# PEER channel mixer: 64 of the 512 prompt tokens through gathered expert rows, the other 448 dense, and group loads in four parts

## The chip, the cores and the metric

One core of one Trainium2 chip runs the whole program in one launch. The metric is the device time of that launch in microseconds. All computing is in fp32; the large products are made of three fp32r products of a high and a low part each (high times high, high times low, low times high).

## What is computed

Two decoder layers on 512 prompt tokens and 8 sample tokens, with a width of 1024. Each layer is a token mixer (a gated MLP in the first, sparse attention in the second) and then PEER, the part that the change touches:

```python
def _peer(h, w_q, sub_k1, sub_k2, expert_u, expert_v):
    ...
        q = (xb @ w_q).reshape(PEER_BLOCK, PEER_HEADS, 2, PEER_HALF)
        s1 = jnp.einsum('thd,kd->thk', q[:, :, 0], sub_k1).astype(jnp.float32)
        s2 = jnp.einsum('thd,kd->thk', q[:, :, 1], sub_k2).astype(jnp.float32)
        v1, i1 = lax.top_k(s1, PEER_TOPK)
        v2, i2 = lax.top_k(s2, PEER_TOPK)
        ...
        top_s, top_pos = lax.top_k(cand, PEER_TOPK)
        eidx = jnp.take_along_axis(cand_idx, top_pos, axis=-1)
        gate = jax.nn.softmax(top_s, axis=-1)
        u = expert_u[eidx]
        act = jax.nn.gelu(jnp.einsum('thkd,td->thk', u, xb))
        vv = expert_v[eidx]
        return jnp.einsum('thk,thkd->td', (gate * act).astype(vv.dtype), vv)
```

Each token has 8 heads, and each head picks 16 of 16384 experts. An expert is one row of `expert_u` and one of `expert_v`, 1024 numbers (4 KB) each.

## The kernel before, in words

The prompt tokens don't gather. For them the kernel computes all 16384 experts densely, since 512 tokens of 128 choices each touch most of them anyway, and multiplies the result by a gate that is zero where an expert was not chosen. The work goes by **slabs**: a slab is 128 experts by 1024, so `expert_u` and `expert_v` have 128 slabs each per layer, and every other weight matrix is cut in slabs too. SyncE (SP) loads slab after slab into four buffers `raw`; ScalarE (ACT) copies one into `w_hi` (`split`, line 937), GpSimd (POOL) subtracts to get `w_lo` (line 1897), and TensorE (PE) makes 24 matmuls of it (8 pieces of the contraction, 3 products), in `dense` (line 517) with 512 token columns each, in `slab` (line 504) with 2 x 260. `w_hi` and `w_lo` have two buffers each, so ACT and POOL work one slab ahead of PE.

A layer's PEER has two stages.

**Stage s** (u rows, 128 slabs): PE's result of a slab goes through the gelu on ACT (line 1045) to HBM (`act_d`). Between slabs the routing runs, for four blocks of 128 tokens: VectorE (DVE) finds the best keys and experts (`routing`) beside 12 slabs of PE, PE turns the result round (line 681), and then 16 slabs follow with a step of gates each: DVE makes one-hot rows of 8 tokens (lines 1535 and 1536), PE multiplies them into the 128 x 128 gate table of each token (`gates`, line 637), ACT evicts it (line 1058), and SP stores it (`gate_d`). 12 + 16 slabs by four blocks are 112; 16 slabs without gates end the stage. The 8 sample tokens are gathered: in blocks 1 and 2 POOL fetches rows of u, then of v, by an indirect DMA (line 1931; 64 rows: 8 heads by 8 tokens), and DVE makes the dot product (line 1512) or adds the weighted row (line 1524).

**Stage y** (v rows, 128 slabs in 16 groups of 8): for each group ACT issues two loads, the activations `abuf` and the gates `gbuf` (lines 1067 and 1069), DVE multiplies them (`weigh`, line 1606), ACT and POOL split the product into `y_hi` and `y_lo` (lines 1081 and 1962; the second set of buffers is `h_hi` and `h_lo`), and PE multiplies with the v slabs; DVE adds each result into `x` (line 1621). The group ahead is prepared while PE works on the present one. The first group is loaded and split at the end of stage s (`load_first`, `hi_part`, `low_part`).

The order on each engine is the order of the code; semaphores alone tie the engines together. What sets the order around the change is written out by hand: the last slabs of stage s and `y_group` on ACT, POOL and DVE:

```python
def hi_part(j, c, par):
    act.wait_ge(y_mult, j * GRP + (W0 + c + 1))
    act.activation(y_hi[par][:, c, 0:TP], abuf[par][:, c, :], ACT.Copy).then_inc(y_hi_done, 1)
```

Of the kernel before, what the change touches and what calls it, by code (L numbers as in the profile page):

```python
# [111 lines left out]
def build(nc, a, outs, layers=2):  # L112
# [3 lines left out]
    with es:  # L116
# [30 lines left out]
        sel_t = sb("sel_t", [SR, TS])  # L147
        ms_at = place[0]
# [58 lines left out]
        idxT = take("idxT", [P, 2, TP])  # L207
        gateT = take("gateT", [P, TP])
# [13 lines left out]
        qS = take("qS", [P, 2, SR])  # L222
        y_tail = take.end
        gelu = take("gelu", [P, 2, TP])
# [5 lines left out]
        rows_at = take.end  # L230
        rows = [take(f"rows{r}", [P, D]) for r in range(2)]
        h_rows = take("h_rows", [P, D])
        v_sum = take("v_sum", [P, D])
        hS = at("hS", [P, KC, SR], F32, ms_at)
# [133 lines left out]
        v_sum_done, s_y_done, s_y_added = sem("v_sum_done"), sem("s_y_done"), sem("s_y_added")  # L368
        stored = sem("stored")
# [31 lines left out]
        N_CONST = 9  # L401
# [4 lines left out]
        def _(sp):  # L406
# [18 lines left out]
            def peer_loads(l, last):  # L425
# [23 lines left out]
                for b in range(4):  # L449
                    steps(12)  # L450
                    q1 = done[0] // 4
                    with sp.Fori(q1, q1 + P // HG // 4, 1) as q:
# [5 lines left out]
                    done[0] += P // HG  # L458
# [30 lines left out]
        def _(pe):  # L489
# [20 lines left out]
            def dense(n, r, par, m_hi, m_lo, free, made=None):  # L510
# [105 lines left out]
            def peer(l):  # L616
# [30 lines left out]
                for j in range(2):  # L647
                    last = pe.matmul(acc[0:SR, 1, 0, j * P:(j + 1) * P], qS[:, j, :], subk[:, 2 * l + j, :],
                                     start=True, stop=True)
                last.then_inc(s_sc_done, 1)  # L650
                for c in range(KC):
                    last = pe.transpose(acc[0:SR, c // 4, 1, (c % 4) * P:(c % 4 + 1) * P], hS[:, c, :], ident[:])
                last.then_inc(h_rows_done, 1)

                for b, (t0, w) in enumerate(BLOCK[:NDB]):
                    B = l * NDB + b
                    if b == 3:
# [3 lines left out]
                        for c in range(KC):  # L661
                            last = pe.matmul(acc[:, 0, 1, c * TS:(c + 1) * TS], v_sum[0:SR, c * P:(c + 1) * P],
# [1487 lines left out]
```

## Time and profile before

| | |
|---|---|
| device time, median of 3 runs | 4435.58 us (4430.29 to 4436.59) |
| the profiled execution's own time | 4438.91 us |
| its span, first to last instruction | 4437.1 us |
| busy PE, DVE, ACT, POOL | 94%, 46%, 32%, 45% |
| mean granted TensorE clock | 0.973 of full speed |
| moved by DMA | 659.83 MB, mean 149 GB/s |

Busy time is the time in which an engine executes at least one instruction; matmuls overlap each other, so the mean length of one (about 0.4 us) is longer than the distance from one to the next, and the distance is what counts. "Idle before" is the time for which an engine stood still ahead of an instruction, with what released it. The queue's own rows (ACTq, SPq) show how long an issue kept the engine's instruction stream.

### The profile page before, as it was taken

The numbers are of one execution on the slowest core, as the hardware profiler recorded it, in microseconds if no ns is written. First come the engines' busy times: TensorE is split into PE (matmuls) and PEld (weight loads), VectorE is DVE, ScalarE is ACT, GpSimd is POOL, SyncE is SP. The second block draws the span as 40 slices with busy tenths as digits, with TensorE's granted clock in tenths as the row PEclk, the third lists the DMA queues.
The fourth block names the chain that finished last, engine by engine and source line by source line (L and its number), as shares of the span: only waits on it lengthen the run. The fifth ranks groups of instructions, "written<-read, shape, count | busy, mean of one in ns | idle before, by whom it ended". The sixth has DMA issues, their size and how long they took to land.

```text
span 4437.1 us, 65563 instructions
## 1 busy us (share of the span) xinstructions
PE 4182.9 (94%) x21677; PEld 3461.8 (78%) x21677; DVE 2052.0 (46%) x5322; ACT 1437.1 (32%) x1929; POOL 1997.9 (45%) x1004
## 2 busy tenths in 40 slices
PE   7899999999998999999887799999999998999998
PEld 7898887878886888887853458887878887888887
DVE  2332567989722222222556432567989721222221
ACT  2222343434432333332220332343434432333332
POOL 3333334444335666665520003334444335666664
PEclk9999999999999999999997899999999999999999
DMA  3122344645457565652134222344645457565652
GB/s 119 67 72 71 105 161 151 205 154 189 146 180 227 183 196 182 201 177 93 62 114 144 74 65 72 102 161 145 206 154 193 148 176 228 187 193 185 198 180 81
DMA packets 345165, 659.83 MB, mean 149 GB/s; under 512 B 22008, under 2 KB 186616, under 8 KB 336248
## 3 DMA queue, kind: packets, MB, share of 16 engines
q1 hardware_dynamic: 163152, 488.74, 32.2%
q10 hardware_dynamic: 176096, 149.67, 11.5%
q0 software_dynamic: 5776, 19.72, 1.9%
q8 instruction: 66, 1.08, 0.1%
q14 instruction: 75, 0.61, 0.0%
HBM read 520.44 MB, written 137.61 MB: 148 GB/s over the span
## 4 chain that ended last, share of the span: by engine, by line
PE 88%; DVE 4%; issue 4%; POOL 2%; ACT 1%; ACTq 0%; DMA 0%; SPq 0%; POOLq 0%; DVEq 0%
PE acc L517 61%; PE acc L504 14%; PE misc L637 5%; PE misc L842 1%; PE acc L856 1%; POOL w_lo L1897 1%; PE misc L879 1%; PE misc L527 1%; PE misc L784 1%; PE acc L868 1%; DVE passed L1733 1%; PE misc L672 1%; DVE sq L1340 1%; DVE hot_gate L1536 0%; DMA unit<-ck_in 0%
## 5 line engine op out<-in xcount | busy, mean ns | idle before, releaser
L1897 POOL TENSOR_TENSOR w_lo<-raw,w_hi 128x1024 fp32r<-128x1024 f32 x620 | 1539.5, 2484 | 2207.5 <-ACT w_hi L937 2207.5
L517 PE MATMUL acc<-h_hi,w_hi 128*128 128x512 f32 x3072 | 1233.0, 401 | 25.9 <-POOL w_lo L1897 25.6
L517 PE MATMUL acc<-h_hi,w_lo 128*128 128x512 f32 x3072 | 1220.0, 397 | 0.0
L517 PE MATMUL acc<-h_lo,w_hi 128*128 128x512 f32 x3072 | 1213.7, 395 | 0.0
L937 ACT ACTIVATE w_hi<-raw 128x1024 fp32r<-128x1024 f32 x620 | 656.9, 1060 | 1310.5 <-PE acc L517 897.5
L517 PEld LDWEIGHTS acc<-h_hi,w_hi 128*128 128x128 f32 x3072 | 579.8, 189 | 164.6 <-issue 35.2
L517 PEld LDWEIGHTS acc<-h_hi,w_lo 128*128 128x128 f32 x3072 | 579.8, 189 | 139.2
L517 PEld LDWEIGHTS acc<-h_lo,w_hi 128*128 128x128 f32 x3072 | 580.8, 189 | 133.7
L1621 DVE TENSOR_TENSOR x<-x,acc 128x512 f32<-128x512 f32 x256 | 176.0, 687 | 1087.2 <-PE acc L517 1087.2
L1045 ACT ACTIVATE gelu<-acc 128x512 f32<-128x512 f32 x256 | 152.9, 597 | 969.3 <-PE acc L517 969.2
L1535 DVE TENSOR_SCALAR hot<-acc,idxT 128x128 f32<-128x128 f32 x1024 | 344.3, 336 | 244.9 <-PE misc L637 129.6
L517 PE MATMUL acc<-y_hi,w_hi 128*128 128x512 f32 x1024 | 402.0, 393 | 29.7 <-POOL y_lo L1962 16.4
L1536 DVE TENSOR_SCALAR hot_gate<-acc,idxT,gateT 128x128 f32<-128x128 f32 x1024 | 405.5, 396 | 0.0
L517 PE MATMUL acc<-y_lo,w_hi 128*128 128x512 f32 x1024 | 401.2, 392 | 0.0
L517 PE MATMUL acc<-y_hi,w_lo 128*128 128x512 f32 x1024 | 400.9, 391 | 0.0
L504 PE MATMUL acc<-h_hi,w_hi 128*128 128x260 f32 x1472 | 311.5, 294 | 79.2 <-DVE h_lo L1343 30.0
L504 PEld LDWEIGHTS acc<-h_hi,w_hi 128*128 128x128 f32 x1472 | 233.5, 194 | 94.3 <-issue 74.0
L504 PE MATMUL acc<-h_hi,w_lo 128*128 128x260 f32 x1472 | 302.8, 288 | 0.0
L504 PE MATMUL acc<-h_lo,w_hi 128*128 128x260 f32 x1472 | 302.6, 288 | 0.0
L1606 DVE TENSOR_TENSOR abuf<-abuf,gbuf 128x512 f32<-128x512 f32 x256 | 181.4, 713 | 225.1 <-DMA gbuf<-gate_d 225.1
L1058 ACT ACTIVATE gout<-misc 128x512 f32<-128x512 f32 x256 | 250.6, 1058 | 35.7 <-PE misc L637 35.7
L637 PEld LDWEIGHTS misc<-hot_gate,hot 128*128 128x128 f32 x2048 | 247.5, 191 | 15.9 <-issue 5.2
(307 smaller groups left out, 4454.1 us busy)
## 6 DMA issues: line engine op xcount, KB each, us to landing
raw<-slabs_in SPq DMA_DIRECT2D x620, 512.0 KB, 3.5
act_d<-gelu SPq DMA_DIRECT2D x256, 256.0 KB, 2.1
gate_d<-gout SPq DMA_DIRECT2D x64, 1024.0 KB
abuf<-act_d ACTq DMA_DIRECT2D x32, 2048.0 KB, 10.9
gbuf<-gate_d ACTq DMA_DIRECT2D x32, 2048.0 KB, 19.0
unit<-cv_in SPq DMA_DIRECT2D x128, 128.0 KB, 2.0
unit<-ck_in SPq DMA_DIRECT2D x64, 160.0 KB, 3.1
unit<-ck_in ACTq DMA_DIRECT2D x64, 160.0 KB, 3.1
```

The costliest lines, as they stand in the source:

```text
L504: last = pe.matmul(acc[:, par, half, 0:HT], w[:, c, :], m(c)[:, half * HT:(half + 1) * HT], start=start and c == 0 and w is w_hi[r] and m ...
L517: last = pe.matmul(acc[:, par, 0, :], w[:, c, :], m(c)[:, 0:TP], start=c == 0 and w is w_hi[r] and m is m_hi, stop=c == KC - 1 and w is w_ ...
L527: last = pe.matmul(misc[:, half, 0:HT], ones[:], sq[:, c, half * HT:(half + 1) * HT], start=c == 0, stop=c == KC - 1)
L637: last = pe.matmul(misc[:, q, j * P:(j + 1) * P], hot1[par][:, t, :], hot_gate[par][:, t, :], start=True, stop=True)
L937: act.activation(w_hi[r % 2][:], raw[r][:], ACT.Copy).then_inc(hi_done, 1)
L1045: act.activation(gelu[:, par, :], acc[:, par, 0, :], ACT.Gelu_apprx_tanh).then_inc(acc_free_act, 1)
L1058: act.activation(gout[cpar][:, :, t0:t0 + 4].rearrange("p i t -> p t i"), misc[:, q, :].rearrange("p (t i) -> p t i", t=4), ACT.Copy).then ...
L1535: dve.tensor_scalar(hot1[par][:, t, :], count_row, idxT[:, 0, t0 + t:t0 + t + 1], None, ALU.is_equal)
L1536: last = dve.tensor_scalar(hot_gate[par][:, t, :], count_row, idxT[:, 1, t0 + t:t0 + t + 1], gateT[:, t0 + t:t0 + t + 1], ALU.is_equal, AL ...
L1606: dve.tensor_tensor(abuf[par][:, c, :].rearrange("p (n t) -> p n t", t=TG), abuf[par][:, c, :].rearrange("p (n t) -> p n t", t=TG), gbuf[p ...
L1621: dve.tensor_tensor(x[:, c, 0:TP], x[:, c, 0:TP], acc[:, c % 2, 0, :], ALU.add).then_inc(acc_free_dve, 1)
L1897: pool.tensor_tensor(w_lo[r % 2][:], raw[r][:], w_hi[r % 2][:].bitcast(F32), ALU.subtract).then_inc(lo_done, 1)
```

## The change

The last 64 prompt tokens (448 to 511) leave the dense path. `ND` is 448: every matmul of `dense`, every gelu, `weigh`, split and addition now has 448 columns, `act_d` and `gate_d` are that much smaller, and block 3 has 8 steps of gates instead of 16 (`STEPS_OF`). The 64 tokens are `NSG` = 4 groups of 16 tokens by 8 heads, 128 partitions. For each group POOL fetches 16 times 128 rows of u and 16 times 128 rows of v into four buffers `rows_p`; the first comes 24 slabs before the end of stage s, and from then on one fetch follows each slab. DVE makes one product with a fetched row per slab (`group_dot`, `group_value`), with the group's tokens, or its sum, in PSUM. The low part of y moves from POOL to DVE (`low_part`). ACT loads a group in four parts, one every second slab, and in stage s it loads the first two groups together. The loops of stage y are written out.

```diff
+ND = 448
+NSG = (TP - ND) // TG
+NG = ND // TG
+RB = 4
...
+                        steps(8)
+                        sp.wait_ge(route_done, l * NDB + 4)
+                        sp.dma_start(route_d[l].rearrange("g t k h s -> (g t) k h s"),
+                                     route[P - NSG * TG:P]).then_inc(p_route_stored, 16)
+                        steps(4)
+                        sp.wait_ge(p_route_stored, 16 * (l + 1))
+                        for g in range(NSG):
+                            for h in range(PH):
+                                sp.dma_start(routeP[h * TG:(h + 1) * TG, g], route_d[l][g, :, :, h]).then_inc(
+                                    p_route_loaded, 16)
...
-                        last = pe.matmul(acc[:, par, 0, :], w[:, c, :], m(c)[:, 0:TP],
+                        last = pe.matmul(acc[:, 0, par, 0:ND], w[:, c, :], m(c)[:, 0:ND],
...
+                def group_h(g):
+                    pe.wait_ge(p_hS_done, l * NSG + g + 1)
...
+                    for c in range(KC):
+                        last = pe.transpose(acc[:, 1, c // 4, (c % 4) * P:(c % 4 + 1) * P], hSP[:, c, :], ident[:])
+                def group_y(g):
+                    pe.wait_ge(p_v_out_done, l * NSG + g + 1)
+                    for c in range(KC):
+                        last = pe.matmul(misc[:, 2, c * TG:(c + 1) * TG], v_out[:, c * P:(c + 1) * P], sel_p[:],
+                                         start=True, stop=True)
...
+                def load_part(j, par, part):
+                    k = part % 2
+                    if part < 2:
+                        act.dma_start(gbuf[par][:, k * NG // 2:(k + 1) * NG // 2],
...
                 def load_first():
                     for par in range(2):
-                        act.wait_ge(act_stored[par], (l * NK // 2 + GRP // 2 + 1) * 16)
+                        act.wait_ge(act_stored[par], (l * NK // 2 + 2 * GRP // 2 + 1) * 16)
                         act.wait_ge(gate_stored[par], ((l + 1) * NG // 2 + 1) * 16)
                     load_group(0, 0)
+                    load_group(1, 1)
...
                 s_only(8)
                 load_first()
-                s_only(4)
+                s_only(8)
+                group_act(0)
+                s_only(NK - 4 - done[0])
...
+            def group_dot(l, g, k):
...
+                dve.wait_ge(p_rows_loaded[i % RB], 16 * (i // RB + 1))
+                row = rows_p[i % RB]
+                dve.tensor_tensor_reduce(out=row[:].rearrange("p (k d) -> p k d", k=2), in0=acc[:, 1],
+                                         in1=row[:].rearrange("p (k d) -> p k d", k=2), scale=1.0, scalar=0.0,
+                                         op0=ALU.mult, op1=ALU.add, accum_out=dotP[:, k:k + 1]).then_inc(p_rows_used, 1)
+            def group_value(l, g, k):
...
+                    dve.wait_ge(p_rows_used, i)
+                    dve.scalar_tensor_tensor(total, row, weightP[:, k:k + 1], total, ALU.mult, ALU.add).then_inc(
+                        p_rows_used, 1)
...
+                for i in range(TOPK):
+                    sparse(i)
                 for c in range(GRP):
-                    weigh(0, 0, c, 0)
+                    weigh(0, c)
+                for c in range(GRP):
+                    sparse(TOPK + c)
+                    low_part(0, c)
...
+                    if TAIL + n < NSG * 2 * TOPK:
+                        sparse(TAIL + n)
+                    if j + 1 < J:
+                        low_part(j + 1, c)
...
+                def group_fetch(i):
+                    g, k = divmod(i, 2 * TOPK)
+                    n = l * NSG * 2 * TOPK + i
+                    if n >= RB:
+                        pool.wait_ge(p_rows_used, n - RB + 1)
...
+                    if n == done:
+                        pool.wait_ge(p_expert_done, l + 1)
+                        for par in range(2):
+                            pool.wait_ge(gate_stored[par], ((l + 1) * NG // 2 + 1) * 16)
+                    while fetched < min(n - done + 3, NSG * 2 * TOPK):
+                        group_fetch(fetched)
+                        fetched += 1
```

How the rows of an engine stand, in three places. The first is DVE in stage y, over one slab, before (`abuf` and `gbuf` are the group's activations and gates, `acc` is PSUM):

```order
L1621 TENSOR_TENSOR x<-x,acc 128x512
L1606 TENSOR_TENSOR abuf_140<-abuf_140,gbuf_141 128x512
L1618 REGISTER_ALU
L1620 REGISTER_ALU
L1621 TENSOR_TENSOR x<-x,acc 128x512
```

and now:

```order
L1789 TENSOR_TENSOR x<-x,acc 128x448
L1745 TENSOR_TENSOR abuf_149<-abuf_149,gbuf_150 128x448
L1645 SCALAR_TENSOR_TENSOR misc<-rows_p_148,weightP,misc 128x1024
L1752 TENSOR_TENSOR h_lo<-abuf_149,h_hi 128x448
L1789 TENSOR_TENSOR x<-x,acc 128x448
```

The product with a fetched row (`misc` is PSUM, `rows_p_148` one of the four row buffers) and the low part stand between `weigh` and the next addition into `x`.

The second is POOL near the end of stage s, now, where the first rows are fetched; before, only the rows of `w_lo` stood here, and `y_lo` behind them:

```order
L2059 TENSOR_TENSOR w_lo_60<-raw_54,w_hi_58 128x1024
L2124 DMA rows_127<-u_in,expertP 128x1024
L2124 DMA rows_128<-u_in,expertP 128x1024
L2124 DMA rows_p_148<-u_in,expertP 128x1024
L2059 TENSOR_TENSOR w_lo_59<-raw_55,w_hi_57 128x1024
L2124 DMA rows_p_151<-u_in,expertP 128x1024
L2059 TENSOR_TENSOR w_lo_60<-raw_56,w_hi_58 128x1024
```

Three fetches follow the first split, and one each of the next 125.

The third is ACT at `load_first`, before (eight slabs behind the last step of gates, and eight ahead of stage y):

```order
L937 ACTIVATE w_hi_57<-raw_53 128x1024
L1042 REGISTER_ALU
L1045 ACTIVATE gelu<-acc 128x512
L1048 REGISTER_ALU
L1048 COMPARE_AND_BRANCH
L1067 DMA abuf_136<-act_d 128x8x512
L1069 DMA gbuf_137<-gate_d 128x32x128
```

and now:

```order
L1002 ACTIVATE w_hi_57<-raw_53 128x1024
L1108 REGISTER_ALU
L1111 ACTIVATE gelu<-acc 128x448
L1114 REGISTER_ALU
L1114 COMPARE_AND_BRANCH
L1135 DMA gbuf_145<-gate_d 128x14x128 x2
L1140 DMA abuf_144<-act_d 128x4x448 x2
L1135 DMA gbuf_150<-gate_d 128x14x128 x2
L1140 DMA abuf_149<-act_d 128x4x448 x2
```

Two loads have become eight, ahead of the next split on ACT; the loads of the second group stood behind the last split of stage s before.

## Rows read from the trace of the kernel before

**Rows 1.** The page, part 1 (busy time) and part 4 (chain that ended last), whole span.

```profile
PE 4182.9 (94%) x21677; PEld 3461.8 (78%) x21677; DVE 2052.0 (46%) x5322; ACT 1437.1 (32%) x1929; POOL 1997.9 (45%) x1004
PE 88%; DVE 4%; issue 4%; POOL 2%; ACT 1%; ACTq 0%; DMA 0%; SPq 0%; POOLq 0%; DVEq 0%
```

**Rows 2.** Stretches: us, busy (x) PE, PEld, DVE, ACT, POOL, PEclk, DMA share, GB/s.

```profile
404.06:490.81 86.75, 86.73 (x720) 86.53 (x720) 9.79 (x14) 14.86 (x14) 35.57 (x15) 1.00 0.28 94
1276.96:1360.68 83.72, 83.72 (x362) 67.57 (x361) 7.11 (x8) 23.69 (x31) 36.58 (x15) 1.00 0.61 203
1400.00:2090.00 690.00, 690.00 (x3002) 562.54 (x3001) 156.29 (x242) 208.23 (x248) 454.02 (x243) 1.00 0.55 174
800.00:840.00 40.00, 40.00 (x224) 34.29 (x223) 40.00 (x100) 18.89 (x23) 17.31 (x11) 1.00 0.62 201
1322.00:1342.00 20.00, 20.00 (x88) 16.12 (x87) 0.00 (x0) 5.94 (x8) 9.11 (x4) 1.00 0.98 318
```

**Rows 3.** Chain of waits, stage s with gates: start us, us, what.

```profile
1210.54 5.59 PE acc L517 x24
1216.14 1.78 PE misc L637 x16
```

**Rows 4.** Timeline of ACT, DVE, POOL, one slab of stage y.

```profile
1804.40 1.06 ACT L937 ACTIVATE w_hi<-raw 128x1024 fp32r<-128x1024 f32 x1 [3.60 <-PE acc L517]
1804.43 0.69 DVE L1621 TENSOR_TENSOR x<-x,acc 128x512 f32<-128x512 f32 x1 [4.29 <-PE acc L517]
1805.03 0.68 DVE L1606 TENSOR_TENSOR abuf<-abuf,gbuf 128x512 f32<-128x512 f32 x1
1805.54 2.44 POOL L1897 TENSOR_TENSOR w_lo<-raw,w_hi 128x1024 fp32r<-128x1024 f32 x1 [1.84 <-ACT w_hi L937]
1807.94 1.28 POOL L1962 TENSOR_TENSOR y_lo<-abuf,y_hi 128x512 fp32r<-128x512 f32 x1
```

**Rows 5.** Timeline of DVE and POOL where they meet: stage s, block 1, and first weigh.

```profile
770.94 1.21 DVE L1512 CUSTOM_DVE_ANT_0 v_sum<-rows,h_rows 64x1024 f32<-64x1024 f32 x1
...
804.76 2.39 POOL L1897 TENSOR_TENSOR w_lo<-raw,w_hi 128x1024 fp32r<-128x1024 f32 x1 [2.74 <-ACT w_hi L937]
805.11 0.39 DVE L1536 TENSOR_SCALAR hot_gate<-acc,idxT,gateT 128x128 f32<-128x128 f32 x1
805.42 2.81 DVE L1512 CUSTOM_DVE_ANT_0 v_sum<-rows,h_rows 64x1024 f32<-64x1024 f32 x1
...
1386.34 2.34 POOL L1897 TENSOR_TENSOR w_lo<-raw,w_hi 128x1024 fp32r<-128x1024 f32 x1 [12.23 <-ACT w_hi L937]
1386.88 2.34 DVE L1606 TENSOR_TENSOR abuf<-abuf,gbuf 128x512 f32<-128x512 f32 x1 [35.98 <-DMA gbuf<-gate_d]
```

**Rows 6.** Timeline from stage s to stage y: ACT's issues, and PE's waits.

```profile
1374.30 8.88 ACTq L1067 DMA_DIRECT2D abuf<-act_d  x1
1383.33 1.65 ACTq L1069 DMA_DIRECT2D gbuf<-gate_d  x1
1385.20 1.06 ACT L937 ACTIVATE w_hi<-raw 128x1024 fp32r<-128x1024 f32 x1 [16.25 <-issue]
...
1374.44 0.79 PE L517 MATMUL acc<-y_hi,w_hi 128*128 128x512 f32 x1 [8.20 <-POOL y_lo L1962]
1388.94 0.79 PE L517 MATMUL acc<-y_hi,w_hi 128*128 128x512 f32 x1 [6.99 <-POOL w_lo L1897]
```

**Rows 7.** DMA issues: queue, count, KB each, median us from issue to landing.

```profile
gbuf<-gate_d ACTq DMA_DIRECT2D x32, 2048.0 KB, 19.0
rows<-u_in,expert POOLq DMA_INDIRECT x32, 4.2
```

**Rows 8.** Timeline of PE and DVE, routing of block 3 beside twelve slabs.

```profile
1086.19 0.48 PE L517 MATMUL acc<-h_hi,w_hi 128*128 128x512 f32 x1
...
1139.75 0.79 PE L517 MATMUL acc<-h_hi,w_hi 128*128 128x512 f32 x1 [3.06 <-POOL w_lo L1897]
1144.58 0.29 DVE L1482 TENSOR_TENSOR route<-route,gsum 128x128 f32<-128x128 f32 x1
```

More of the change, by code:

```diff
@@ L147, in build @@
         sel_t = sb("sel_t", [SR, TS])
+        sel_p = sb("sel_p", [P, TG])
         ms_at = place[0]
@@ L222, in build @@
         qS = take("qS", [P, 2, SR])
+        idxT = take("idxT", [P, 2, ND])
+        gateT = take("gateT", [P, ND])
         y_tail = take.end
-        gelu = take("gelu", [P, 2, TP])
+        gelu = take("gelu", [P, 2, ND])
+        gates_at = take.end
         HG = TG // 2
@@ L228, in build @@
         gout = [take(f"gout{r}", [P, P, TG]) for r in range(2)]
-        rows_at = take.end
+        gates_end = take.end
         rows = [take(f"rows{r}", [P, D]) for r in range(2)]
@@ L233, in build @@
         v_sum = take("v_sum", [P, D])
+        h_sp = at("h_sp", [P, KC, NSG * TG], F32, take.end - 2 * 4 * D)
+        v_out = v_sum
+        routeP = take("routeP", [P, NSG, 3, TOPK])
+        expertP = take("expertP", [P, NSG, TOPK], U32)
+        dotP = take("dotP", [P, TOPK])
+        dot_actP = take("dot_actP", [P, TOPK])
+        weightP = take("weightP", [P, TOPK])
+        hSP = at("hSP", [P, KC, P], F32, ms_at)
         hS = at("hS", [P, KC, SR], F32, ms_at)
@@ L1954, in peer @@
                     done += P // HG
-                plain(q0 + done // 4, (NK - 4 - done) // 4)
-                done = NK - 4
-                W0 = l * NK
-                J = NK // GRP
-                def low_part(j, c, par):
-                    pool.wait_ge(y_hi_done, j * GRP + (W0 + c + 1))
-                    pool.tensor_tensor(y_lo[par][:, c, 0:TP], abuf[par][:, c, :], y_hi[par][:, c, 0:TP].bitcast(F32),
-                                       ALU.subtract).then_inc(y_lo_done, 1)
-                for r in range(4):
-                    ahead(q0 + done // 4, r)
-                    if r >= 2:
-                        for c in range(GRP // 2):
-                            low_part(0, (r - 2) * GRP // 2 + c, 0)
@@ L1971, in peer @@
-                yq0 = BASE[f"y{l}"] // 4
-                def y_group(j, par, last):
-                    for c in range(GRP):
-                        ahead(j * 2 + (yq0 + c // 4), c % 4, last=l == LAST_L and last and c == GRP - 1)
-                        if not last:
-                            low_part(j + 1, c, 1 - par)
-                with pool.Fori(0, J - 2, 2) as j:
-                    y_group(j, 0, False)
-                    y_group(j + 1, 1, False)
-                y_group(J - 2, 0, False)
@@ new lines, in peer @@
+                fetched = 0
+                for n in range(done, 2 * NK):
+                    ahead(q0 + n // 4, n % 4, last=l == LAST_L and n == 2 * NK - 1)
+                    if n == done:
[5 more added lines that the diff above has]
+                        fetched += 1
```

251 lines of the change are left out of this document (171 added, 80 removed).

## The prediction

> **What bounds the kernel now.** I read the page first, then stretches of each stage, then the chain and the timelines where stages meet. PE is busy for 94% of the span and holds 88% of the chain that ended last [rows 1]. The stretches say how: in 690 us of stage y PE issues 3002 matmuls without a gap, one per 0.230 us, 5.52 us for the 24 of a slab; in the last fifteen plain slabs of stage s it is 83.72 us / 15 = 5.58 us [rows 2]. A slab with gates adds 1.78 us, in 16 records of 0.111 us [rows 3]. So what counts is PE's column count, as long as every other engine finishes within a slab. In stage y they do: ACT splits 1.06 us, POOL 2.44 + 1.28 us, DVE 0.69 + 0.68 us [rows 4]. Little else stops PE; where it stands still, I count it below.
>
> A difference of under 0.2%, 9 us, a measurement of this kernel can't tell from none. The profiled execution took 4438.9 us; the sum is made against it, and the median of the runs shown is 3 us lower.
>
> **The columns.** All 512 slabs of both stages in both layers go from 512 to 448 columns. At 260 columns a matmul follows another after 86.75 us / 720 = 0.1205 us, at 512 after 83.72 / 360 = 0.2326 us [rows 2]. Between them lies 0.000445 us per column, so 64 columns are worth 0.0285 us, 24 matmuls 0.68 us: a slab takes 4.90 us in stage s and 4.84 us in stage y. 512 x 0.68 = **-350 us**. Strict proportion would give 0.70 us and -356.
>
> The Trainium skill (VectorE: DVE Perf Modes, on the TRN2 errata) gives a matmul 6 cycles plus one per column at 2.4 GHz: 64 columns would be 0.0267 us and the term an estimated -328. By its formula 512 columns are 0.216 us; the trace has 0.2326, so I go by the trace's slope.
>
> **The gates.** Block 3 has 8 steps less per layer: 16 x 1.78 = **-28 us** [rows 3]. Their slabs stay, as plain ones.
>
> **PE's new work.** Four groups per layer, each with 8 transposes and 8 small matmuls. The nearest rows are the fp32 matmuls of the gates, 0.111 us per record, two records each [rows 3]: at most 16 x 0.222 = 3.6 us, at least half, since a transpose or 16 columns may need less. I take 2.5 us, eight times: **+20 us** (14 to 28).
>
> **From stage s to stage y.** Before, PE waits 8.20 us for the first `y_lo` and 6.99 us for a `w_lo` [rows 6]. The second wait is ACT's: with one group's loads outstanding, the next issue held its queue 8.88 us, the one behind it 1.65 us, and `w_hi` came 16.25 us late. Each time the matmuls after the wait come at half speed (0.79 us the first) for some 3 us, 1.5 us lost. Together 18 us a layer. Now that wait moves rather than goes. `load_first` issues both groups, eight parts, between two splits. Two groups were 8.4 MB, and are 7.3 MB now, so I scale the 15.9 us between ACT's last split and its next to 12 to 13 us. Then 1.06 us `w_hi` and 2.4 us `w_lo` follow, against a slab of 4.9 us in progress: PE waits about 11 us, half speed behind it. If the queue takes smaller parts without holding, eight issues of about 0.5 us each cost nothing to 3 us.
> At the stage's end a new wait follows from the order of DVE: its second value row stands behind `low_part(0, 0)`, which needs `y_hi` of slab 124; POOL's fetch of row 21 waits for that value before POOL splits the next slab. From slab 124's end that is gelu 0.6, `y_hi` 0.6, `low_part` 0.6, value 1.2, then `w_lo` 2.4 us: PE waits some 5.5 us. And group 0 is complete only when DVE has made its last two low parts and a value, about 4 us after slab 127. 11 + 5.5 + 4 + three restarts of 1.5 = 25 to 26 us against 18: **+16 us** for both layers (-30 to +40).
>
> **POOL's wait for the gate stores.** Before the first fetches POOL waits for the last 1 MB gate store, issued about 2 us after PE's last gates step, and then issues three fetches of 0.9 us or more. The next `w_lo` is due within that slab: 3 to 5 us of PE per layer, **+8 us** (0 to 16).
>
> **Block 3 and SP.** SP now waits for `route_done` after 8 of the 12 slabs. DVE finishes routing 58.4 us after PE's first matmul of the block [rows 8]. Twelve new slabs take 58.8 us, so DVE is just in time, where it had 14 us. But SP stands at that wait with the gelu stores of slabs 8 and later and the load of slab 12 behind it; gelu 10 needs store 8 landed. That makes slab 12 late by 2 to 7 us: **+10 us** for two layers. The 32 small loads of `routeP` (0.35 us each as SP issues, 11 us) pass beside two slabs with gates. DVE's copy and sum of the 64 tokens ahead of the first one-hot rows, 2 us, and the first step of gates in each block now shows behind a shorter slab: **+10 us**.
>
> **Routing collisions.** POOL's `w_lo` is held by a long DVE instruction, and PE waits 3.06 us [rows 8]. With 0.68 us less per slab, each of eight blocks loses about 1 us more: **+8 us**.
>
> **DVE and POOL in stage y.** DVE gets a product of 128x1024 and the low part. The price of the product is the question. Alone, the sample dot takes 1.21 us; started beside POOL's `w_lo` (804.76 to 807.15) it takes 2.81, from 805.42 to 808.23, which is the wait for POOL's end plus its own time. `weigh` does the same at 1386.88. One-hot rows, whose big input is PSUM, keep 0.39 us beside POOL [rows 5]. So two SBUF inputs wait for POOL, and the change keeps the other operand of the product in PSUM: 1.2 to 1.3 us, in any place. DVE per slab: 0.55 + 0.6 + 1.25 + 0.55 = 2.95 us, of which `weigh` runs before POOL starts (1.1 us into the slab) and `low_part` after it ends (3.6 us): done at 4.2 us of 4.84. POOL: 2.44 + fetch 0.9 (64 rows) to 1.8 us. Both fit. The slack of 0.6 us fails at some group ends, where PE needs all low parts, above all because `weigh` runs twice in a group's first slab: 0.6 us each in 32 groups, **+20 us** (0 to 60).
> The Trainium skill (SBUF — State Buffer, Who interferes with whom) has this as a rule: a VectorE instruction with two SBUF inputs and a GpSimd one that reads SBUF exclude each other for a whole instruction, one SBUF input does not. The rows agree.
>
> **Sum.** -350 - 28 + 20 + 16 + 8 + 10 + 10 + 8 + 20 = -286: 4438.9 - 286 = 4153, less 3 for the median: **4150 us**, chance 0.50.
>
> **The rivals.**
> *The stalls shrink.* The queue takes the small parts, and the transition gets better than before (-30), the group ends fit (0), the small terms halve: about -365, **4075 to 4100**. For it: parts of 0.9 MB; against it: the 8.88 us [rows 6]. Chance 0.17.
> *DMA is the bound of stage y.* A slab now needs 512 KB of weights, 512 KB of rows, and 448 KB of group: 1.51 MB in 4.84 us, 311 GB/s, where 174 are moved now. With everything queued, the trace holds 318 GB/s for 20 us at a share of 0.98 [rows 2], with more small packets than later. The present group takes 19 us to land [rows 7]; a fetch has about 7 us from issue to use, and 64 rows land in 4.2. At 285 GB/s a slab is 5.29 us: 208 slabs x 0.45 = +94, **4245 us** (300 GB/s: +39; 265 GB/s: +176). Chance 0.20.
> The Trainium skill (DMA: Bandwidth & Descriptors, Specifications) puts HBM at about 358 GB/s per core; by that 311 fits, at 87%.
> *The product waits for POOL after all (slower).* If the custom dot, or a sum that is read and written in PSUM, needs the same port, all of `w_lo` 2.44, `weigh` 0.6, the product 1.2, `low_part` 0.55 and the fetch 0.9 to 1.8 us exclude each other: 5.7 to 6.6 us, and with a hand-over between two in-order engines at each step 6.5 us. Then 208 slabs x 1.66 = +345: **4495 us**. From 6.2 us per slab on the change loses. For it: the product was never run on PSUM in this trace; against it: the one-hot rows. Chance 0.08.
> *It doesn't buy columns.* If 128 weight rows at 0.188 us per load were the floor rather than the columns, 448 columns would save nothing: about 4500 us. Against it: 260 columns follow at 0.1205. Chance 0.01; the rest, 0.04, is for mixtures above 4300.
>
> **The numbers.** Range 4080 to 4290: it holds the likeliest case with its bounds, most of the first rival, and the DMA case to 270 GB/s. Faster by over 0.2%: 0.89, within: 0.02, slower: 0.09.
>
> **What would show it.** Plain slabs of stage s at 4.9 us; 16 gate records gone from 16 steps; the product at 1.2 to 1.3 us beside POOL; ACT's queue held for about 12 us at `load_first`, with one PE wait of 11 us; PE busy in stage y with gaps at group ends only. I am wrong if stage y's slabs come at over 5.1 us, with DVE waiting for rows or parts (DMA) or with products of over 2 us (the port).

## The result and the profile after

The changed kernel takes **4130.39 us** (median of 4 runs, 4124.94 to 4132.71). The kernel before took 4436.09 us beside it (4 runs, 4430.29 to 4442.36). The ratio is 0.9309, with a 95% interval of 0.9293 to 0.9325: 306 us less. The profiled execution took 4132.7 us, its span is 4130.9 us, and the mean granted TensorE clock is 0.967.

The page of the changed kernel, parts 1 and 4, answers to [rows 1]:

```profile
PE 3827.7 (93%) x21613; PEld 3464.5 (84%) x21613; DVE 2661.3 (64%) x5734; ACT 1366.3 (33%) x1913; POOL 1954.2 (47%) x1004
PE 81%; DVE 7%; issue 5%; POOL 2%; ACT 2%; SPq 1%; DMA 1%; ACTq 0%; POOLq 0%; DVEq 0%
```

PE's busy time fell by 4182.9 - 3827.7 = 355.2 us. The time in which PE is idle rose from 4437.1 - 4182.9 = 254.2 to 4130.9 - 3827.7 = 303.2 us. So PE's smaller work brings 355 us, and 49 us of new waits are taken off it.

Two stretches of the changed kernel, stage s without gates and stage y, answer to [rows 2]. Columns: us, busy (x) of PE, PEld, DVE, ACT, POOL, PEclk, DMA share, GB/s.

```profile
1230.00:1275.00 45.00, 45.00 (x223) 41.64 (x222) 15.61 (x19) 14.11 (x21) 30.61 (x18) 1.00 0.82 257
1600.00:1680.00 80.00, 80.00 (x402) 74.50 (x401) 68.32 (x70) 25.57 (x33) 59.44 (x34) 1.00 0.90 310
```

PE is busy without a gap in both. In y DVE is busy for 68.32 of 80 us, and the DMA engines move 310 GB/s where they moved 174. One slab of y in the changed kernel, timeline of DVE and POOL, answers to [rows 4]:

```profile
1450.84 2.69 DVE L1745 TENSOR_TENSOR abuf<-abuf,gbuf 128x448 f32<-128x448 f32 x1
1453.45 1.28 DVE L1645 SCALAR_TENSOR_TENSOR misc<-rows,weightP,misc 128x1024 f32<-128x1024 f32 x1
1454.64 0.61 DVE L1752 TENSOR_TENSOR y_lo<-abuf,y_hi 128x448 fp32r<-128x448 f32 x1
1455.18 0.61 DVE L1789 TENSOR_TENSOR x<-x,acc 128x448 f32<-128x448 f32 x1
1455.71 2.69 DVE L1745 TENSOR_TENSOR abuf<-abuf,gbuf 128x448 f32<-128x448 f32 x1
...
1450.64 2.41 POOL L2059 TENSOR_TENSOR w_lo<-raw,w_hi 128x1024 fp32r<-128x1024 f32 x1 [1.16 <-ACT w_hi L1002]
1453.20 1.16 POOL L2124 DMA_INDIRECT rows_p<-v_in,expertP  x1 [0.15 <-issue]
```

From one `weigh` to the next are 4.87 us: that is a slab. `weigh` starts 0.2 us behind `w_lo`, lasts until POOL has ended, and ends 0.48 us after that. The product that follows has its sum in PSUM and takes 1.28 us.

The new waits stand where the stages meet. Timeline of ACT and of PE in the first layer, end of stage s, answering to [rows 6]:

```profile
1194.56 1.35 ACTq L1135 DMA_DIRECT2D gbuf<-gate_d  x2
1195.94 7.80 ACTq L1140 DMA_DIRECT2D abuf<-act_d  x2
1203.77 6.63 ACTq L1135 DMA_DIRECT2D gbuf<-gate_d  x2
1210.43 4.35 ACTq L1140 DMA_DIRECT2D abuf<-act_d  x2
1215.06 1.06 ACT L1002 ACTIVATE w_hi<-raw 128x1024 fp32r<-128x1024 f32 x1 [20.22 <-issue]
...
1218.77 0.74 PE L554 MATMUL acc<-h_hi,w_hi 128*128 128x448 f32 x1 [19.64 <-POOL w_lo L2059]
```

`load_first`'s eight issues keep ACT for 20 us. `w_hi` comes late, `w_lo` behind it, and PE stands 19.64 us (19.96 in the second layer). Some 65 us later, in the last slabs of stage s, timelines of DVE, POOL and PE:

```profile
1280.33 0.62 DVE L1752 TENSOR_TENSOR y_lo<-abuf,y_hi 128x448 fp32r<-128x448 f32 x1 [19.15 <-ACT y_hi L1158]
1280.87 1.28 DVE L1645 SCALAR_TENSOR_TENSOR misc<-rows,weightP,misc 128x1024 f32<-128x1024 f32 x1
...
1282.42 1.08 POOL L2124 DMA_INDIRECT rows<-v_in,expertP  x1 [8.92 <-DVE misc L1645]
1283.53 2.35 POOL L2059 TENSOR_TENSOR w_lo<-raw,w_hi 128x1024 fp32r<-128x1024 f32 x1
...
1286.11 0.74 PE L554 MATMUL acc<-h_hi,w_hi 128*128 128x448 f32 x1 [6.86 <-POOL w_lo L2059]
...
1300.33 0.46 PE L554 MATMUL acc<-h_hi,w_hi 128*128 128x448 f32 x1 [2.00 <-POOL w_lo L2059]
```

DVE's second value stands behind a low part that waits for ACT's `y_hi`; POOL's fetch waits for the value, and the split of the next slab for the fetch. A last place is block 3, where SP first waits for `route_done` and then issues the 32 loads of `routeP`, timelines of SP and PE:

```profile
1092.07 20.95 SPq L486 DMA_DIRECT2D routeP<-route_d  x32
...
1092.24 0.46 PE L554 MATMUL acc<-h_hi,w_hi 128*128 128x448 f32 x1 [3.84 <-POOL w_lo L2059]
```

### The profile page after: what moved, and what is told of

Its sections match the earlier page's. It is cut to its first block, busy times and chain, and to the rows that moved or that the text cites. A ratio compares the mean times of both kernels' runs of the same rounds, so it can differ in the third digit from the quotient of the medians.

```text
span 4130.9 us, 64131 instructions
## 1 busy us (share of the span) xinstructions
PE 3827.7 (93%) x21613; PEld 3464.5 (84%) x21613; DVE 2661.3 (64%) x5734; ACT 1366.3 (33%) x1913; POOL 1954.2 (47%) x1004
## 4 chain that ended last, share of the span: by engine, by line
PE 81%; DVE 7%; issue 5%; POOL 2%; ACT 2%; SPq 1%; DMA 1%; ACTq 0%; POOLq 0%; DVEq 0%
PE acc L554 52%; PE acc L541 15%; PE misc L674 5%; POOL w_lo L2059 2%; PE misc L907 1%; PE acc L921 1%; SPq L486 1%; PE misc L849 1%; PE misc L944 1%; PE misc L564 1%; PE acc L933 1%; DVE passed L1895 1%; DMA act_d<-gelu 1%; PE misc L709 1%; DVE sq L1423 1%
## 5 line engine op out<-in xcount | busy, mean ns | idle before, releaser
L554 PE MATMUL acc<-h_hi,w_hi 128*128 128x448 f32 x3072 | 1143.9, 372 | 100.3 <-POOL w_lo L2059 100.3
L554 PE MATMUL acc<-h_hi,w_lo 128*128 128x448 f32 x3072 | 1130.7, 368 | 0.0
L554 PE MATMUL acc<-h_lo,w_hi 128*128 128x448 f32 x3072 | 1127.2, 367 | 0.0
L554 PEld LDWEIGHTS acc<-h_hi,w_lo 128*128 128x128 f32 x3072 | 582.9, 190 | 47.7
L554 PEld LDWEIGHTS acc<-h_lo,w_hi 128*128 128x128 f32 x3072 | 584.0, 190 | 45.6
L1111 ACT ACTIVATE gelu<-acc 128x448 f32<-128x448 f32 x256 | 139.3, 544 | 852.8 <-PE acc L554 806.2
L554 PE MATMUL acc<-y_hi,w_hi 128*128 128x448 f32 x1024 | 372.4, 364 | 5.2 <-DVE y_lo L1752 5.2
L554 PE MATMUL acc<-y_lo,w_hi 128*128 128x448 f32 x1024 | 372.6, 364 | 0.0
L554 PE MATMUL acc<-y_hi,w_lo 128*128 128x448 f32 x1024 | 371.8, 363 | 0.0
L1789 DVE TENSOR_TENSOR x<-x,acc 128x448 f32<-128x448 f32 x256 | 158.5, 619 | 223.8 <-PE acc L554 207.6
L541 PEld LDWEIGHTS acc<-h_lo,w_hi 128*128 128x128 f32 x1472 | 233.6, 194 | 0.0
L541 PEld LDWEIGHTS acc<-h_hi,w_lo 128*128 128x128 f32 x1472 | 232.9, 193 | 0.0
```

What stands on the lines that cost most here:

```text
L541: last = pe.matmul(acc[:, par, half, 0:HT], w[:, c, :], m(c)[:, half * HT:(half + 1) * HT], start=start and c == 0 and w is w_hi[r] and m ...
L554: last = pe.matmul(acc[:, 0, par, 0:ND], w[:, c, :], m(c)[:, 0:ND], start=c == 0 and w is w_hi[r] and m is m_hi, stop=c == KC - 1 and w is ...
L1111: act.activation(gelu[:, par, :], acc[:, 0, par, 0:ND], ACT.Gelu_apprx_tanh).then_inc(acc_free_act, 1)
L1789: dve.tensor_tensor(x[:, c, 0:ND], x[:, c, 0:ND], acc[:, 0, c % 2, 0:ND], ALU.add).then_inc(acc_free_dve, 1)
```

## The experiments

All twelve start from the changed kernel and alter one thing, or join such alterations. Times are medians; the ratio is to the kernel before, measured beside each (its medians: 4433.6 to 4435.0 us).

**1. Loads of the first groups spread out (load_spread).**

The edit, shortened:

```diff
 load_first()    # now without its two load_group calls
-load_group(0, 0); load_group(1, 1)    # they stood in load_first
-s_only(8)
+for i in range(8):
+    s_step(done[0] // 4 + i // 4, i % 4)
+    load_part(i // 4, i // 4, i % 4)
```

> Edit: the eight loads with which ScalarE fetches groups 0 and 1 of a layer go out one after each of the next eight slabs of the s stage instead of all in a row; nothing else changes. Theory 1 (ScalarE's queue is held by its own loads): in the changed kernel TensorE stands 19.64 us (first layer) and 19.96 us (second) before the matmul at 1218.77, while ScalarE's issues and weight truncations in that place take 1.35, 7.80, 6.63 and 4.35 us plus 20 us of idle put down to issue. Spread out, each load has a slab of 4.87 us to go, the gap falls to under 3 us in both layers, and the time is 4130 - 2 x (17 to 19) = 4092 to 4097 us. Theory 2 (the loads move as fast as the DMA engines allow, whoever issues them, and the wait only moves to where the group is first used): a new gap of 10 to 20 us shows before the first slabs of y, and the time stays within 4120 to 4132 us.

Measured: 4100.18 us, ratio 0.9249 (0.9235 to 0.9263), 30 us less. ACT and PE in its timeline:

```profile
1204.36 5.20 ACTq L1140 DMA_DIRECT2D abuf<-act_d  x1
...
1213.40 0.47 PE L554 MATMUL acc<-h_hi,w_hi 128*128 128x448 f32 x1 [4.21 <-ACT w_hi L1002]
```

Nothing new shows at the start of y (2.61 us, as without the edit). ACT's queue was the cause. One load in each slab is still too many: the third, activations behind two loads of gates, holds ACT for 5.20 us.

**2. Values ahead of the low parts (values_first).**

```diff
 for c in range(GRP):
     sparse(TOPK + c)
+for c in range(GRP):
     low_part(0, c)
```

> Edit: at the end of the s stage VectorE adds the eight weighted rows 16 to 23 of group 0 first and then makes the eight low parts of dense group 0; in the changed kernel it takes them in turns. Theory 1 (the turns tie the fetches on GpSimd to ScalarE's last slabs: a fetch waits for a row to come free, the row for a low part ahead of it, that for y_hi, that for the last gelus): the gap of 6.86 us before the matmul at 1286.11 goes in each layer, and the restart at half clock behind it; time 4130 - 2 x (6 to 9) = 4112 to 4118 us. Theory 2 (the low parts are then late at the start of y, 8 x 0.6 us in a row on VectorE): the 2.61 us before 1310.49 grow to 6 to 9 us and the time stays at 4125 to 4135 us.

Measured: 4099.92 us, ratio 0.9247 (0.9234 to 0.9259), 30 us less, about twice what I expected. The wait of 6.86 us is gone, 0.30 us is left of the one of 2.00, and 2.24 us are left before y (2.61 before). From the end of `load_first`'s wait to the first matmul of y PE now takes 78.6 us instead of 91.7, and 79.1 instead of 92.8 in the second layer: 27 us less, of which 17 are waits and the other 9 to 10 are the clock. What is left of the 30 lies outside of the edit's reach and is not explained. Timeline of PE in the **changed** kernel:

```profile
1286.11 0.74 PE L554 MATMUL acc<-h_hi,w_hi 128*128 128x448 f32 x1 [6.86 <-POOL w_lo L2059]
1286.64 0.57 PE L554 MATMUL acc<-h_lo,w_hi 128*128 128x448 f32 x1
...
1291.46 0.37 PE L554 MATMUL acc<-h_hi,w_hi 128*128 128x448 f32 x1
1291.67 0.37 PE L554 MATMUL acc<-h_lo,w_hi 128*128 128x448 f32 x1
...
1301.26 0.57 PE L554 MATMUL acc<-h_lo,w_hi 128*128 128x448 f32 x1
1301.63 0.57 PE L554 MATMUL acc<-h_hi,w_lo 128*128 128x448 f32 x1
```

Behind the long wait the matmuls come every 0.37 us instead of 0.20, up to 1291; behind the wait of 2.00 us the clock falls a second time, 0.9 us after the matmuls have begun again. The granted clock is 0.50 from 1286 to 1290 and 0.66 from 1300 to 1305: 1.2 GHz for 4.6 and for some 3.5 us. It falls a third time behind the wait before y. In all 31 matmuls come at the slow distance here, and 8 in run 2. So such a wait costs its length and 1.5 to 2 us more, but not each does: behind the 2.37 us before 547.61 us the matmuls keep the full clock, and behind the 2.37 us before 1071.63 us the clock falls in the changed kernel and doesn't in run 2.

**3. Routes in eight stores and one load (route).**

The edit, shortened (the layout of `route_d` and DVE's wait for the loads change with it):

```diff
-steps(8); wait route_done; 1 store [g, t, k, h, s]; steps(4); 32 loads
+steps(12)
+sp.wait_ge(route_done, l * NDB + 4)
+for h in range(PH):
+    sp.dma_start(route_d[l][:, h], route[P - NSG * TG:P, :, h, :]).then_inc(p_route_stored, 16)
+sp.dma_start(routeP[:], route_d[l].rearrange("g h t k s -> (h t) g k s")).then_inc(p_route_loaded, 16)
```

> Edit: the 64 tokens' routes go out to DRAM in eight stores that already put the heads in order, behind 12 slabs of block 3 instead of 8, and come back in one load in place of 32. Theory 1 (SyncE's queue decides here: it stood 3.84 us for the routing at 1092.24, and the 32 small loads held it for 20.95 us, in which slab 1123.81 waited for its store): the gap of 3.84 us goes, those at 1119.39 and 1123.81 (0.58 and 2.38) go or shrink to the 2.4 us of the other blocks, and the time falls by 2 x (4 to 7) us to 4116 to 4122 us. Theory 2 (the eight stores with 32-byte pieces and the wait for them hold SyncE as long as the 32 loads did): no change, 4127 to 4133 us.

Measured: 4114.17 us, ratio 0.9282 (0.9269 to 0.9294), 16 us less, slightly more than expected. SP's rows in its timeline:

```profile
1084.90 4.03 SPq L481 DMA_DIRECT2D route_d<-route  x7
1090.54 0.40 SPq L483 DMA_DIRECT2D routeP<-route_d  x1
```

The 20.95 us are gone and so are PE's waits of 3.84, 0.58 and 2.38 us in the block; one of 1.97 us before a gates step is new. From the last wait ahead of the block's end (1071.63 us in the changed kernel) to the one behind it the run takes 6.6 us less, and 6.0 in the second layer; 9 of these 12.6 us are waits. The other 3 to 4 us of the 16 are not explained; the stretch up to 1071.63 us, which no edit touches, took 5.2 us less in this profiled execution.

**4. The three together (three).**

> Edit: the edits of load_spread, values_first and route together. If the three waits are independent, the gains add: 2 x (18 + 7 + 5) = 60 us, 4070 us (4058 to 4082). If they are one wait that passes from one place to the next, the sum is under 60 per cent of what the three bring alone, and the time stays above 4090 us. If TensorE's matmul stream were not the bound of the stages, gaps of over 1 us would show inside the slabs of y, where the changed kernel has none.

Measured: 4061.13 us, ratio 0.9155 (0.9142 to 0.9167). Alone they bring 30, 30 and 16, 76 in all; together 69, over 90% of it: the waits are independent but for 7 us.

**5. The product with both operands in SBUF (dot_sbuf).**

The edit, shortened; the sums are then of row times row, and everything else stays:

```diff
-dve.tensor_tensor_reduce(out=row, in0=acc[:, 1], in1=row, ...
+dve.tensor_tensor_reduce(out=row, in0=row,       in1=row, ...
```

> Edit: the product of a fetched row with the token's vector takes the row twice, both operands from SBUF, in place of PSUM and SBUF (the sums are then of row times row; everything else is as before). The question is what the operand in PSUM buys. Theory 1 (a VectorE instruction with two SBUF operands and GpSimd's split or fetch do not run together, one with an operand in PSUM does): a slab of y with a dot then has 2.41 (w_lo) + 1.16 (fetch) + 0.54 + 0.54 (weigh, low part) + 1.2 (dot) = 5.85 us one after the other against 4.87 us of matmuls; 48 such slabs in each layer give 96 x 1.0 = 96 us more, 4215 to 4280 us. Theory 2 (where the operands lie does not matter here, the order of the queues alone does): 4125 to 4140 us.

Measured: 4136.65 us, ratio 0.933 (0.9316 to 0.9344), 6 us more, with intervals that still overlap (the changed kernel's ends at 0.9325). The mechanism of theory 1 is there, its price is not. DVE and POOL in its timeline, stage y:

```profile
1399.98 1.21 DVE L1625 CUSTOM_DVE_ANT_0 rows_p<-rows_p 128x1024 f32<-128x1024 f32 x1
1405.12 3.42 DVE L1625 CUSTOM_DVE_ANT_0 rows_p<-rows_p 128x1024 f32<-128x1024 f32 x1
...
1399.95 3.49 POOL L2059 TENSOR_TENSOR w_lo<-raw,w_hi 128x1024 fp32r<-128x1024 f32 x1
1404.89 2.56 POOL L2059 TENSOR_TENSOR w_lo<-raw,w_hi 128x1024 fp32r<-128x1024 f32 x1
```

One of the two now waits for the other: at 1400 the split takes 3.49 us beside a product of 1.21, at 1405 the product 3.42. Over y the mean product takes 2.04 us instead of 1.22. So the operand in PSUM does keep the product and the split apart. Only the products with u rows were edited, 96 of them in y; the 112 with v rows kept their sum in PSUM. But the slab holds it: without the fetch the exclusive pieces are 2.41 + 0.54 + 0.54 + 1.21 = 4.70 us, under 4.87. My 5.85 had counted the fetch, 1.16 us, as one of them; run 8 shows places where it isn't, this run also fetches of 1.76 us that start within such a product.

**6. One load every second slab (spread_two).** Like run 4, with `s_only(4)` ahead of `load_first` and `load_part` after every second of the next 16 slabs.

> Edit: like three, but the eight loads start four slabs earlier and go out one every second slab. In load_spread TensorE still stood 4.21 and 4.87 us, since the third load (of 896 KB) took ScalarE 5.20 us to issue. Theory 1 (a slab of s with a fetch moves 512 KB of weights, 224 KB of acts and 512 KB of rows, 1.25 MB; a load more in every slab makes 2.14 MB in 4.87 us, 440 GB/s, above the 300 to 400 the trace shows at its highest; one every second slab makes 1.7 MB, 348 GB/s): the gap of 5 us goes or falls under 2 us in both layers, 4061 - 2 x (4 to 7) = 4047 to 4053 us. Theory 2 (group 1 then lands too late for the first slabs of y): the gap turns up at the start of y, 4060 to 4075 us.

Measured: 4044.50 us, ratio 0.9123 (0.9111 to 0.9136), 86 us under the changed kernel. Each of the eight issues now takes 0.37 to 0.42 us, and from slab 108 to the start of y PE waits 0.30 us once; the wait before y's first matmul stays (2.67 us).

**7. Without the sparse work (no_sparse).** All calls of `group_fetch`, `sparse`, `group_h`, `group_act`, `group_out`, `group_y`, `group_add` and `group_rows` are left out.

> Left out: everything that is done for the 64 sparse tokens behind their routes (fetches, products, gelus, the transposes and the last matmuls on TensorE, the additions), so that their rows of the output lack the layer's part. Theory 1 (TensorE's columns bound both stages and the sparse work lies beside them): the distance of the matmuls in y stays 0.203 us and a slab 4.87 us; the time falls only by TensorE's own new work (8 groups x 2.6 = 21 us) and by the waits at the end of s (2 x 15, as values_first showed) and in the group changes: 4060 to 4080 us. Theory 2 (the fetches or VectorE's products slow the slabs of y): slabs of y get under 4.8 us and the time falls under 4040 us.

Measured: 4076.77 us, ratio 0.9197 (0.9183 to 0.9211): 54 us under the changed kernel. The slabs of y gain nothing beyond PE's own work: from 1400 to 1800 us PE is busy without a gap in both, and a slab takes 4.83 to 4.84 us on average, once PE's transposes and sums are taken off, with rows, products and 307 GB/s as without them and with 204. The wait for `load_first` stays. ACT and PE in its timeline:

```profile
1188.34 6.86 ACTq L1135 DMA_DIRECT2D abuf<-act_d  x2
...
1210.19 0.74 PE L554 MATMUL acc<-h_hi,w_hi 128*128 128x448 f32 x1 [18.63 <-POOL w_lo L2040]
```

There is no fetch here, so the fetches don't cause it.

**8. Fewer columns in y (y384).** `dense` of stage y takes `0:384` instead of `0:ND`; nothing else changes.

> Left out: the matmuls of y run over 384 of the 448 dense columns, so that 64 tokens get no sum; all loads, splits, weighings and sparse work stay. The question is what bounds y next. From 512 to 448 columns the distance of the matmuls went from 0.230 to 0.203 us, so 384 columns would be 0.176 us and a slab 4.22 us. Theory 1 (VectorE and the DMA engines have room for that): 256 x 0.65 = 166 us less, 3960 to 3970 us. Theory 2 (GpSimd and VectorE take turns: 2.41 + 1.16 + 0.54 + 0.54 = 4.65 us in each of the 104 slabs a layer that still have sparse work): 208 x 0.22 + 48 x 0.65 = 77 us less, about 4053 us. Theory 3 (the DMA engines, which moved 306 GB/s in y, have no more): slabs with a fetch stay at 4.87 us, only the 48 others gain, about 4099 us.

Measured: 4024.75 us, ratio 0.9071 (0.9056 to 0.9085), 106 us less: between theories 1 and 2. The distance of the matmuls is 0.175 us and most slabs take 4.21 us, as theory 1 has it; the rest is lost at the group changes. Its waits from 1400 to 1800 us (us in total, times, longest) and two rows of its timelines of POOL and DVE:

```profile
PE acc L554 <- DVE h_lo L1752: 9.0, 6, 2.1
PE acc L554 <- DVE x L1789: 6.0, 12, 0.7
DVE rows_p L1625 <- DMA rows_p<-u_in,expertP: 13.2, 9, 2.2
...
1514.82 0.95 POOL L2124 DMA_INDIRECT rows_p<-u_in,expertP  x1
1515.09 0.08 DVE L1625 DVE_READ_ACCUMULATOR2_ANT dotP<- 128x1 f32 x1
1515.09 0.62 DVE L1752 TENSOR_TENSOR y_lo<-abuf,y_hi 128x448 fp32r<-128x448 f32 x1
```

Theory 2 falls as a floor of 4.65 us in each slab: the low part at 1515.09 runs wholly beside a fetch, and takes its own 0.62 us. What comes next is DVE at the group changes, and behind it the rows, for which DVE now waits up to 2.2 us while 329 GB/s are moved at a DMA share of 0.95 (1400 to 1600 us). Whether the rows are late because the DMA engines are nearly full, no run settles. Theory 3 falls too.

**9. The four loads of a group in a burst (burst).**

```diff
-if j + 2 < J and c % 2 == 0:
-    load_part(j + 2, par, c // 2)
+if j + 2 < J and c == 0:
+    load_group(j + 2, par)
```

> Edit: in y the four loads of a later group go out all before its first slab instead of one every second slab; the rest is as in the changed kernel. Theory 1 (ScalarE is held when it issues loads faster than they land): the weights and rows of a slab take 1.04 MB in 4.87 us, 213 GB/s, of the 300 to 400 seen, so four loads of 0.9 MB need 20 to 30 us; ScalarE is free again when the third and fourth have room, 5 to 10 us late, in each of 14 groups of 2 layers: 140 to 280 us more, 4270 to 4410 us. Theory 2 (ScalarE's one or two slabs of lead and the queue's depth take them, as they did with the two loads per group of the kernel before): 4125 to 4140 us.

Measured: 4366.14 us, ratio 0.9839 (0.9822 to 0.9856), 236 us more: theory 1, within its range. ACT's rows for one group in its timeline:

```profile
1406.83 1.29 ACTq L1135 DMA_DIRECT2D gbuf<-gate_d  x2
1408.15 7.12 ACTq L1140 DMA_DIRECT2D abuf<-act_d  x2
1415.38 1.06 ACT L1002 ACTIVATE w_hi<-raw 128x1024 fp32r<-128x1024 f32 x1 [11.08 <-issue]
```

PE then stands 4.6 to 7.5 us in each group, and its busy time rises by 61.6 us for the same matmuls, since the clock falls behind each such wait.

**10. Two whole loads, gates first (two_whole).** `load_group` issues `gbuf[par][:]` and then `abuf[par][:]`, in y at `c == 0` and in `load_first`; DVE waits for 32 in place of 64.

> Edit: the four loads of a group are two again (gates whole, activations whole, 1.8 MB each), both before the group's first slab, as in the kernel before; at the end of s the four loads of groups 0 and 1 go out in a row. Theory 1 (the queue counts bytes or descriptors that have not landed): at the end of s ScalarE is held as long as with eight parts, 18 to 20 us, and in y it is held in each group as with the burst of four parts, 4270 to 4410 us. Theory 2 (it counts issues): the wait at the end of s falls under 5 us and y has none, 4130 - 30 = 4095 to 4105 us. Theory 3 (it is held only by loads behind two others): the end of s stays at 18 to 20 us, y has no wait, 4125 to 4140 us.

Measured: 4327.23 us, ratio 0.9759 (0.9741 to 0.9777): theory 1's range, though bytes and pieces aren't told apart yet. ACT in its timeline:

```profile
1444.64 0.38 ACTq L1145 DMA_DIRECT2D gbuf<-gate_d  x1
1445.05 7.41 ACTq L1147 DMA_DIRECT2D abuf<-act_d  x1
```

**11. The same two loads, activations first (act_first).** Run 10 with the two issues exchanged: the order of the kernel before.

> Edit: two_whole with the order turned: activations whole first, gates whole second, as the kernel before has them. In two_whole the gates (3584 pieces of 512 B) were issued in 0.4 us and held the activations behind them (1024 pieces of 1792 B) for 7.4 to 8.1 us; in the kernel before, activations then gates took 0.38 and 0.47 us. Theory 1 (it is the number of small pieces ahead in the queue that holds the next issue; with the gates last nothing stands behind them until the next group, 39 us later): both issues of a group take under 1 us in y, TensorE waits for nothing there, and the end of s still stands 8 to 20 us for group 1: 4100 to 4140 us. Theory 2 (it is the bytes outstanding, 3.6 MB at a time): y is held as in two_whole, 4320 us. Theory 3 (the issues are free but the burst crowds out the weights of the next slabs, since rows need the engines too now): TensorE waits for w_hi or w_lo behind a late raw slab, 4150 to 4250 us.

Measured: 4120.53 us, ratio 0.9292 (0.9278 to 0.9306): theory 1. ACT in its timeline, stage y and end of s:

```profile
1460.84 0.37 ACTq L1145 DMA_DIRECT2D abuf<-act_d  x1
1461.24 0.61 ACTq L1147 DMA_DIRECT2D gbuf<-gate_d  x1
...
1191.52 0.59 ACTq L1147 DMA_DIRECT2D gbuf<-gate_d  x1
1192.14 12.17 ACTq L1145 DMA_DIRECT2D abuf<-act_d  x1
```

The same bytes in the other order cost 207 us less. What follows the gates (3584 pieces of 512 B) at once is held; what follows the activations (1024 pieces of 1792 B) is not. With the gates last, only an issue soon behind them pays: the one at 1192.14 is held until 12.8 us after the gates went out. Bytes outstanding are ruled out. Whether it is the number of the pieces, their size or the way in which `gate_d` is read isn't told apart, since all three change with the order.

**12. Whole loads at two places (whole_two_places).** Run 11 with the edits of runs 2 and 3, group 0 loaded behind slab 108 and group 1 behind slab 116.

> Edit: spread_two with whole loads in place of parts: group 0 (activations, gates) behind slab 108, group 1 behind slab 116, later groups before their first slab, and the order of the values and the routes as in three. If the number of small pieces ahead is what holds ScalarE and the bursts crowd out nothing, this simpler version comes to the 4044 us of spread_two (4040 to 4050). If the bursts delay raw slabs or rows in y, it stays above 4060 us. If bytes outstanding hold it, 4230 us.

Measured: 4047.68 us, ratio 0.9133 (0.9121 to 0.9146), the same as run 6 within the intervals. Stretch of stage y:

```profile
1400.00:1800.00 400.00, 400.00 (x2008) 372.74 (x2007) 326.16 (x361) 127.33 (x169) 284.74 (x157) 1.00 0.88 303
```

No part of a group has to be loaded by itself: the order of two loads does what four parts and an issue every second slab did.

## Why the prediction was right, and where its steps were not

The time, 4130 us, is 20 us under the forecast of 4150 and in its likeliest case. The large term, the columns, came out by its mechanism. That the small terms also met is in part luck: the transition cost twice what was forecast, and 28 us of forecast waits were not there. By its steps:

- **The columns** (-350): right. The slab is 4.87 us in stage s and 4.80 to 4.88, on average 4.84, in y; forecast were 4.90 and 4.84: 256 x (5.58 - 4.87) + 256 x (5.52 - 4.84) = 356 us. With the gates (-28) and PE's new work (+20) I had -358; PE's busy time fell by 355, with more matmuls at half clock in it. The -328 by the Trainium skill's formula (VectorE: DVE Perf Modes) would have been 28 us short for the columns.
- **PE's new work** (+20): right, a group's transposes hold the next slab's matmuls for 0.79 us and its sums for 1.70, 8 x 2.5 = 20.
- **The transition** (+16): the mechanism was right, `load_first` was sized wrongly. I scaled 15.9 us by bytes and wrote 12 to 13 (by 7.3 and 8.4 MB it is 13.8); ACT is held 20.2 us and PE 19.64 instead of 11. The step that failed is "two groups were 8.4 MB, and are 7.3 MB now". Runs 10 and 11 show that not bytes count but what stands ahead of an issue: the gates' many small pieces. All waits of the transition and the stage's end are 62.6 us for both layers, where they were 30.4: +32 without the restarts, inside the stated -30 to +40. The rival in which the small parts are taken without holding fell with the changed kernel's 20.2 us and with run 1's 5.20; with the order of run 6 its price holds.
- **The end of stage s**: the chain from `y_hi` to the fetch was right, 6.86 us for 5.5, and group 0's last low parts cost 2.61 us for 4. A second wait of 2.00 us was not foreseen. With the matmuls at half clock run 2 brings 13 to 14 us a layer at this place.
- **Block 3 and SP** (+10): the wait at `route_done` is there, 3.84 us, in the forecast 2 to 7. Wrong was that the 32 small loads take "0.35 us each as SP issues, 11 us" and pass beside two slabs: they take 20.95 us, 0.65 each, and PE waits 0.58 and 2.38 us behind them. Altogether 16 us could be had (run 3).
- **First steps of gates** (the second +10): there, but small. PE waits 0.90 to 0.96 us for DVE in front of them, 0.2 to 0.3 before: some 4 us in all.
- **POOL's gate-store wait** (+8): smaller, 1.99 us of PE a layer.
- **Routing collisions** (+8): not there. Each block of the first layer now has two waits beside its routing, of 0.53 to 0.79 and 2.37 to 2.52 us, 3.0 in all; before it was one of 2.6 to 3.1.
- **DVE's order in y**: wrong, without a price. `weigh` was to run before POOL starts; it starts 0.2 us behind `w_lo` and is held until POOL ends, 2.69 us. DVE still gets through in 4.87 us.
- **The group changes of y** (+20): not there, PE has no gap in y. DVE is late by nothing at 4.87 us; at 4.21 (run 8) it would be, by up to 2.1 us.
- **DMA as the bound** (rival): fell. 306 to 310 GB/s are moved in y, the 311 needed; run 7 gets no faster slab without the rows, and run 8 moves 329. By its own sum the range held this case to 273 GB/s, not to 270.
- **The product waits for POOL** (rival): fell. It takes 1.22 and 1.28 us. Run 5 takes the PSUM operand away: the wait appears and costs 6 us. That was for 96 of the rival's 208 slabs; at its 1.66 us each they would have cost 159. The slab has room for the pieces that do exclude each other, 4.70 us without the fetch.

Stalls were forecast as 72 us in all; PE's idle time grew by 49, and the clock (0.967 for 0.973) took a part that is counted as busy.

## What to carry to other kernels

Price a narrower matmul by the distances of two widths in the trace, and then look at what each queue has to issue in the shorter slab: here the columns gave 356 us, and changes of the order of issue and of work gave back 86 us (run 6). Put the DMA with the many small pieces last in its burst and keep the next issue of that engine away from it, since the engine that issues is held, not the DMA. Where two in-order engines feed one another, put what waits for nothing ahead of what waits; and count a wait of TensorE above its length where the trace shows slow matmuls behind it, as here behind each wait of run 9 (4.6 to 7.5 us) and behind some of 2.0 to 2.4 us.

## What was not expected of the hardware

- Behind 3584 pieces of 512 B, or two times 1792, the next issue of the same engine takes 5.2 to 12.2 us; behind 1024 pieces of 1792 B 0.6 us. Which number of pieces sets the limit, and whether it is their number or their size, was not measured.
- A wait of only 2.00 us was followed, 0.9 us after the restart, by matmuls at 0.37 us: the second fall of the clock in 15 us. Another of 2.37 us was not. Between run 12 and the changed kernel PE's busy time differs by 3827.7 - 3805.9 = 22 us for the same 21613 matmuls, and the mean clock by 0.977 to 0.967: a quarter of the 89 us of span that it gained is clock.
- The DMA engines moved 400 GB/s from 1218.7 to 1223.0 us in the changed kernel, above the estimate of 358 for HBM in the Trainium skill (DMA: Bandwidth & Descriptors, Specifications). That was a burst; no stage held it. The DMA share is 1.06 in that stretch, above the whole, so the profile's figure is rough there.
- An indirect fetch on POOL (0.95 us) and a VectorE subtraction with two SBUF inputs (0.62 us) ran wholly beside each other in run 8, each in its own time; where POOL's split and such an instruction met, nearly always one of them took longer. In run 5 a fetch that started while VectorE was in a product with both operands in SBUF took 1.76 us. Why the one is free and the other not, no run here settles.
